# A hybrid attention and MLP block on 8 cores: transposing two spilled operands by crossbar DMA, folding their scales into weights, and loading weights in pieces that wait for TensorE

## The chip, the cores and the metric

One Trainium2 chip, all 8 NeuronCores. Each core takes one batch element's half (every second tile of 128 rows, 2048 query rows), and no core talks to another. The metric is device microseconds of the slowest core; a smaller number is better. Of an execution, the span is the time from the first to the last instruction of the slowest core.

## The reference, cut to what matters

```python
xn = rmsnorm(x, norm_mix_g);  u = xn @ w_in               # 1024 -> 5120
b_g, c_g, v_a, q, k, v, gates = split(u)
y_a = (b_g * conv3(c_g * v_a)) @ w_a_out                   # causal depthwise conv, 512 channels
p = softmax(q k^T / 8 + alibi, causal)                     # 4 heads, two maps of 64 each
o = rmsnorm((p[0] - lam * p[1]) @ v, subln_g) * (1 - lam_init)
y_b = o @ w_b_out
x = x + (sig(gate_a) * y_a + sig(gate_b) * y_b) @ w_o
h = rmsnorm(x, norm_mlp_g) @ w_mlp_in                      # 1024 -> 4096
x = x + square(relu(h)) @ w_mlp_out
return rmsnorm(x, norm_final_g)                            # x is (4, 4096, 1024) float32
```

## The kernel before

Sizes. A core's 4096 rows are eight blocks of 512: blocks 0 to 3 are its own queries, 4 to 7 the other core's rows, needed for k and v. The queries are worked on in four groups g of 512 rows (block g). Weights arrive as float32 and are cast to bf16 by the DMA on POOL's queue (`cload`, `wload`); activations, residual tiles and spills go through SP's queue (`ld` and the stores). Both are in-order queues: an instruction that waits holds what stands behind it.

How the order comes about. Python code records instructions per engine in the order in which it runs; `Sched` adds the waits (last writer, readers) and each engine then executes its list in order. A DMA is an instruction on its issuing engine, with the waits of its source, its destination, and of the DMA 24 places earlier on the same queue.

Stages. First k and v of blocks 4 and 0 and q of block 0 (`until(0)`), which need xT (the transposed x), the weights wk, wv, wq, and the rows' sums of squares (`stats`: ACT squares four x tiles, POOL takes the power). Then the attention loop runs over 160 pairs: group, head, and key tile index j; each pair is 8 q.k matmuls, their exps on ACT and 16 p.v matmuls or fewer. Groups have 16, 32, 48 and 64 pairs. Into this stream `other` puts one chunk of other work per pair from the list W: k, v, q of later blocks, the conv branch, and from the third or fourth pair of group 3 on the gated merge G of groups 0, 1, 2. While attention runs, all of W's chunks share one PSUM bank (`oring` is bank 7); after it there are eight.

The merge of one group i (`G_list`): 32 chunks for 8 output tiles dm (`gate_chunks`: gate 0, branch 0 from y_a, gate 1, branch 1 from the attention output), then the loads for the next group (`g_loads`: xn; `g_loads2`: attention output and y_a), then for each of 4 row tiles two z matmul chunks (`z_chunks`, w_o and the residual). A z of 8 matmuls is followed by L792 on DVE (residual added, x tile loaded by SP), then the copy L795, the square on ACT, and the store of x to xm_sp. After the last pair, what is left of W is worked off alone; at that point the merge of group 1 has its z chunks to do, and groups 2 and 3 all.

Two operands are transposed by TensorE before. The attention output of a head (512 rows x 128) in `epilogue`: step `d3` makes four transposes (L722) of `e_b`, DVE empties them with the scale subln_g folded in (L725), and SP stores the result to on_sp, from where `g_loads2` loads it. The x for the MLP: step `tr` of `z_chunks` makes eight transposes of `g_xb` (L806), DVE empties them with norm_mlp_g folded in (L808), and SP stores them to x2_sp, from where `m_load` loads four pieces.

MLP: 4 blocks, each 32 chunks `m_in` (8 matmuls, W1) and 8 chunks `m_out` (32 matmuls, W2). W1 is loaded into the space of a head's k and v when that head of group 3 is done (two DMAs of 1 MB as written a head, `w1_load`), W2 behind attention and behind the merge in 4 DMAs.

The softmax here doesn't subtract the row's maximum and nothing guards it: scores larger than these inputs give would overflow.

## Time and profile before

| | us |
|---|---|
| median of 3 runs | 1470.52 (1470.09 to 1471.43) |
| profiled execution, device time | 1470.92 |
| its span on the slowest core (core 7) | 1469.4 |
| spans of the 8 cores | 1444.3 to 1469.4 |
| TensorE busy in the span | 1214.9 (83%), 7202 matmuls |
| ACT busy, DVE busy, POOL busy | 546.1, 501.7, 63.2 |
| POOL's DMA queue, SP's DMA queue | 39.91 MB, 76.53 MB as written |

The profile gives for each engine the time it was busy, what it waited for and for how long, and the DMAs with the time from issue to landing. A matmul and its weight load are separate rows (PE and PEld). The granted clock of TensorE is 1.00 at 2.4 GHz and 0.50 at 1.2 GHz; a value between is a mean over a stretch. A wait for several things is put down to the one that came last. The rows that are used are shown further down.

### The profile page before, as it was taken

What the parts mean: (1) busy time and instruction counts of PE and PEld (TensorE: products, weight loads), DVE (VectorE), ACT (ScalarE), POOL (GpSimd) and SP (SyncE); (2) the same over time, 40 slices, a digit from 0 to 9 for tenths busy, and PEclk for the clock granted to TensorE, in tenths of its full rate; (3) what the DMA queues carried; (4) which work ended last, traced back from release to release, by engine and by line L of the source; (5) the groups of instructions that cost most, each with busy time, mean ns of one, the idle gap of its engine ahead of it and who ended that gap; (6) DMA issues with size and microseconds to landing.
All of it is one profiled execution on the core that took longest, in us unless ns stands there. A gap on an engine that the chain in (4) does not pass through costs nothing.

```text
span 1469.4 us, 20538 instructions; the slowest of 8 cores (1444.3 to 1469.4 us)
## 1 busy us (share of the span) xinstructions
PE 1214.9 (83%) x7202; PEld 583.9 (40%) x7202; DVE 501.7 (34%) x1087; ACT 546.1 (37%) x744; POOL 63.2 (4%) x97
## 2 busy tenths in 40 slices
PE   3877687888799872898689629895999999999997
PEld 1333343444444441444344204342444444444443
DVE  2354453553445441324232424543212212212212
ACT  1334264647556561566456102221311311311310
POOL 2001000000000000000000000000000000000000
PEclk8877777999999996999899859998999999999999
DMA  9935113122207107044312561518500200201101
GB/s 172 239 82 103 62 41 97 62 54 65 51 4 148 44 15 147 1 90 124 111 23 68 101 201 32 201 22 208 157 24 35 86 21 38 86 19 40 58 16 56
DMA packets 33124, 117.76 MB, mean 80 GB/s; under 512 B 3680, under 2 KB 8032, under 8 KB 29568
## 3 DMA queue, kind: packets, MB, share of 16 engines
q0 software_dynamic: 7200, 39.91, 16.4%
q1 hardware_dynamic: 25824, 76.53, 15.1%
q8 instruction: 60, 0.98, 0.3%
q14 instruction: 40, 0.33, 0.1%
HBM read 126.98 MB, written 29.36 MB: 106 GB/s over the span
## 4 chain that ended last, share of the span: by engine, by line
PE 68%; DMA 11%; DVE 10%; issue 5%; ACT 4%; POOL 1%; DVEq 0%; SPq 0%; ACTq 0%; POOLq 0%
PE ps_all L396 67%; ACT big L662 3%; DMA x_sp<-big 3%; DMA big<-xs 3%; DMA big<-ya_sp 2%; DMA big<-x_sp 1%; DVE big L769 1%; DVE big L686 1%; DMA on_sp<-big 1%; DMA big<-wk 1%; DVE big L705 1%; PE ps_all L806 1%; DVE big L725 1%; DVE big L714 1%; POOL big L710 0%
## 5 line engine op out<-in xcount | busy, mean ns | idle before, releaser
L396 PE MATMUL ps_all<-big 128*128 128x512 bf16 (+3 forms) x7010 | 1201.0, 338 | 164.6 <-DMA big<-ya_sp 28.9
L396 PEld LDWEIGHTS ps_all<-big 128*128 128x128 bf16 (+1 forms) x7010 | 572.2, 101 | 786.7 <-issue 349.4
L662 ACT ACTIVATE big<-ps_all,big 128x1024 bf16<-128x1024 f32 (+3 forms) x384 | 337.9, 926 | 181.2 <-PE ps_all L396 173.5
L879 ACT ACTIVATE big<-ps_all 128x512 bf16<-128x512 f32 x128 | 76.4, 597 | 141.7 <-PE ps_all L396 141.7
L880 DVE TENSOR_TENSOR big<-big 128x512 bf16<-128x512 bf16 x128 | 54.5, 426 | 159.1 <-ACT big L879 158.8
L758 ACT ACTIVATE big<-ps_all,big 128x512 f32<-128x512 f32 x64 | 44.0, 687 | 151.2 <-PE ps_all L396 151.1
L769 DVE SCALAR_TENSOR_TENSOR big<-big,ps_all 128x512 f32<-128x512 f32 x64 | 44.0, 687 | 156.7 <-PE ps_all L396 156.5
L896 ACT ACTIVATE big<-big 128x1024 bf16<-128x1024 f32 x16 | 16.9, 1057 | 208.2 <-DVE big L891 208.2
L891 DVE SCALAR_TENSOR_TENSOR big<-ps_all,big 128x512 f32<-128x512 f32 x32 | 24.0, 751 | 162.9 <-PE ps_all L396 162.9
L796 ACT ACTIVATE big<-big 128x1024 bf16<-128x1024 f32 x16 | 16.9, 1057 | 128.6 <-DVE big L792 128.6
L806 PE MATMUL ps_all<-big 128*128 128x128 bf16 x128 | 10.9, 235 | 55.0 <-DVE big L795 54.2
L440 ACT ACTIVATE big<-big 128x1024 bf16<-128x1024 f32 x32 | 33.8, 1057 | 52.0 <-DMA big<-xs 51.6
L792 DVE SCALAR_TENSOR_TENSOR big<-ps_all,big 128x512 f32<-128x512 f32 x32 | 22.1, 690 | 80.2 <-DMA big<-xs 47.2
L667 DVE TENSOR_TENSOR big<-big 128x256 bf16<-128x256 bf16 x64 | 18.6, 290 | 71.6 <-ACT big L662 71.2
L710 POOL TENSOR_TENSOR big<-big 128x4 f32<-128x4 f32 x16 | 16.4, 1022 | 512.5 <-DVE big L708 441.3
L548 DVE TENSOR_SCALAR big<-ps_all,big 128x512 bf16<-128x512 f32 x32 | 23.7, 750 | 35.1 <-PE ps_all L396 35.1
L806 PEld LDWEIGHTS ps_all<-big 128*128 128x128 bf16 x128 | 8.4, 105 | 61.4 <-issue 61.4
L598 DVE TENSOR_TENSOR big<-ps_all,big 128x512 f32<-128x512 f32 x16 | 11.1, 691 | 57.0 <-PE ps_all L396 57.0
L722 PE MATMUL ps_all<-big 128*128 128x128 bf16 x64 | 6.5, 228 | 26.5 <-DVE big L714 26.4
L898 POOL TENSOR_TENSOR big<-big 128x1 f32<-128x1 f32 x16 | 8.9, 554 | 435.1 <-DVE big L897 435.1
L669 DVE TENSOR_SCALAR big<-big 128x256 bf16<-128x256 bf16 x64 | 18.2, 285 | 26.0 <-ACT big L662 25.9
L808 DVE TENSOR_TENSOR big<-ps_all,big 128x1024 bf16<-128x1024 bf16 x16 | 19.6, 1225 | 17.8 <-DMA x_sp<-big 10.4
(69 smaller groups left out, 362.8 us busy)
## 6 DMA issues: line engine op xcount, KB each, us to landing
big<-xs SPq DMA_DIRECT2D x48, 512.0 KB, 6.1
big<-w POOLq DMA_DIRECT2D x8, 1024.0 KB, 14.6
xm_sp<-big SPq DMA_DIRECT2D x16, 512.0 KB, 4.5
big<-xm_sp SPq DMA_DIRECT2D x16, 512.0 KB, 5.3
out<-big SPq DMA_DIRECT2D x16, 512.0 KB, 2.7
big<-xT POOLq DMA_DIRECT2D x14, 512.0 KB, 11.0
xn_sp<-big SPq DMA_DIRECT2D x4, 1024.0 KB, 4.9
big<-wg POOLq DMA_DIRECT2D x4, 1024.0 KB, 18.2
```

Source lines behind the costliest of these rows:

```text
L396: S.op("pe", lambda e: e.matmul(out, lhsT, rhs, start=start, stop=stop, skip_group_check=skip), reads, writes)
L440: act(lambda e: e.activation(junk.ap, xt.ap, AF.Square, accum_out=ss1[blk].ap[:, t:t + 1]), [xt], [junk, ss1[blk]])
L548: dve(lambda e: e.tensor_scalar_mul(v_all[:, :, n, 0:128], ps.rearrange("p (h v) -> p h v", h=4), rs1[blk].ap[:, t:t + 1]), [key, rs1[blk] ...
L662: act(lambda e, a=a, b=b, c=c, s=s, PT=PT, scale=scale: e.activation(PT.ap[:, :, a:b], Sb[s][:, :, a:b], AF.Exp, bias=ccol(C_BTAB + c), sc ...
L758: act(lambda e: e.activation(t.ap, ps, AF.Tanh, bias=hbg.ap[:, 8 * w + dm:8 * w + dm + 1], scale=0.5), [key, hbg], [t])
L769: dve(lambda e: e.scalar_tensor_tensor(t.ap, t.ap, 1.0, ps, ALU.add, ALU.mult), [key, t], [t])
L792: dve(lambda e: e.scalar_tensor_tensor(x.ap[:, hs], ps, 0.5, x.ap[:, hs], ALU.mult, ALU.add), [key, x], [x])
L806: S.op("pe", lambda e, c=c: e.transpose(pb[:, c, :], g_xb.ap[:, c * 128:(c + 1) * 128], ident), [g_xb, cbf], [key])
L808: dve(lambda e: e.tensor_tensor(g_x2.ap, pb, ccol(C_GMLP, 8).unsqueeze(2).to_broadcast([128, 8, 128]), ALU.mult), [key, cst], [g_x2])
L879: act(lambda e: e.activation(r.ap, ps, AF.Relu), [key], [r])
L880: dve(lambda e: e.tensor_tensor(h2[fc].ap, r.ap, r.ap, ALU.mult), [r], [h2[fc]])
L891: dve(lambda e: e.scalar_tensor_tensor(x.ap[:, hs], ps, r2q[b].ap[:, t:t + 1], x.ap[:, hs], ALU.mult, ALU.add), [key, x, r2q[b]], [x])
```

## The change

Five things are done, all in one diff.

1. The head's output is no longer transposed in the epilogue: `e_b` (now two buffers) is stored as it is, rows by channels, to on_sp, and `g_loads2` loads it with one transposing DMA on SP (`dma_start_transpose`, 512 x 512 to 128 x 4 x 512). The scale subln_g goes into w_b_out: `fold_sub`, four DVE instructions. `g_on` and `g_ya` have buffers of their own.
2. The MLP's x is no longer transposed in the merge: `g_xb` (two buffers) is stored to xb_sp, and `m_load` is one transposing DMA (512 x 1024 to 128 x 8 x 512). norm_mlp_g goes into W1: 64 DVE instructions, spread over time (`w1_steps`).
3. Weight and xT loads on POOL are cut into halves or quarters, recorded at separate places, and each waits for the matmul that stands last in TensorE's order at that point (`paced`). W2's loads are cut in two-tile pieces, not paced; its first six tiles and `m_load(0)` are recorded in the merge behind attention.
4. The start: the x tiles of blocks 4 and 0 go through POOL's queue in a set order (wk and xT of block 4, x of block 4, wv, xT of 0, wq, x of 0, xT of 5).
5. `g_loads2(0)` is recorded 16 pairs before group 3, in place of at the merge's start; the merge may start at pair 98, before at pair 99. `deferred` steps now also run between the chunks behind attention, and are not flushed at its end.

```diff
@@ Sched
-    def _add(self, eng, fn, reads, writes, is_dma):
-        writers, wars = set(), set()
+    def _add(self, eng, fn, reads, writes, is_dma, extra=(), part=False):
+        writers, wars = set(extra), set()
...
+        self.last[eng] = ev
...
@@ build_program
-    def cload(dst, src, bufs, after=()):
-        S.dma("pool", lambda e: e.dma_start(out=dst, in_=src), reads=after, writes=bufs)
+    def cload(dst, src, bufs, paced=False, part=False):
+
+        S.dma("pool", lambda e: e.dma_start(out=dst, in_=src), writes=bufs, extra=[S.last["pe"]] if paced else (),
+              part=part)
...
         def d2():
-            dve(lambda e: e.tensor_tensor(e_b.ap, o[:, 0, :, 0:128],
+            b = e_b.next()
+            dve(lambda e: e.tensor_tensor(b.ap, o[:, 0, :, 0:128],
                                           est.ap[:, 16:20].unsqueeze(2).to_broadcast([128, 4, 128]), ALU.mult),
-                [o_raw, est], [e_b])
-
-        def d3():
-            ps, key = obank()
...
-                S.op("pe", lambda e, t=t: e.transpose(pb[:, t * 128:(t + 1) * 128], e_b.ap[:, t, :], ident),
-                     [e_b, cbf], [key])
...
+                [o_raw, est], [b])
+            dst = on_sp[g].rearrange("(t p) c -> p t c", p=128)[:, :, h * 128:(h + 1) * 128]
+            S.dma("sp", lambda e: e.dma_start(out=dst, in_=b.ap), [b], ["onsp%d_%d" % (g, h)])
+        deferred.extend([(1, d0), (2, d1), (5, d2)])
...
     def g_loads2(i):
-        ld(span(g_on), on_sp[i], g_on, ["onsp%d_%d" % (i, h) for h in range(4)])
-        ld(span(g_ya), ya_sp[i], g_ya, ["yasp%d_%d" % (i, h) for h in range(4)])
+        ld(g_ya.ap.rearrange("p c t -> p (c t)"), ya_sp[i], [g_ya], ["yasp%d_%d" % (i, h) for h in range(4)])
+        S.dma("sp", lambda e: e.dma_start_transpose(g_on.ap, on_sp[i]),
+              ["onsp%d_%d" % (i, h) for h in range(4)], [g_on])
...
                 if half == 1:
-                    dve(lambda e: e.tensor_copy(g_xb.ap, x.ap), [x], [g_xb])
+                    xb = g_xb.next()
+                    dve(lambda e: e.tensor_copy(xb.ap, x.ap), [x], [xb])
...
+                    S.dma("sp", lambda e: e.dma_start(out=xb_sp[T * 128:(T + 1) * 128, :], in_=xb.ap),
+                          [xb], ["xbsp%d" % T])
...
-        def tr():
...
     def m_load(b):
-        x2 = m_x2[b % 2]
-        for t in range(4):
-            ld(x2.ap[:, t].rearrange("p c t -> p (c t)"), x2_sp[b][t], [x2], ["x2sp%d_%d" % (b, t)])
+        S.dma("sp", lambda e: e.dma_start_transpose(m_x2[b % 2].ap, xb_sp[512 * b:512 * (b + 1), :]),
+              ["xbsp%d" % T for T in range(4 * b, 4 * b + 4)], [m_x2[b % 2]])
...
+    def pieces(bufs, src, c0, width, n=2):
...
+    def xT_steps(blk, s):
+        def first():
+            slot_of[blk] = s
+        steps = [lambda q=q: cload(span(XT[s][2 * q:2 * q + 2]), xT_d[blk][:, 1024 * q:1024 * (q + 1)],
+                                   XT[s][2 * q:2 * q + 2], paced=True) for q in range(4)]
...
-    W += [(0, g_w1)] + [(1, f) for f in conv(3)]
+    W += spread(conv(3), pieces([Wa], wa_d, 0, 4096) + pieces([Wb], wb_d, 0, 4096)
+                + pieces(Wg[0:2], wg_d, 0, 4096) + pieces(Wg[2:4], wg_d, 4096, 4096))
...
-    W += [(1, f) for f in conv(2)] + [(0, g_w2)]
+    W += [(1, f) for f in conv(2)] + [(0, fold_sub)]
     mark("G")
-    W += [(0, lambda: g_loads2(0))]
-    W += G_list(0, 1) + G_list(1, 2) + G_list(2, 3)
+    late = pieces(Wg[4:6], wg_d, 8192, 4096) + pieces(Wg[6:8], wg_d, 12288, 4096) + pieces([Wo], wo_d, 0, 8192, 4)
+    g0 = G_list(0, 1)
+    for k, f in enumerate(late):
+        g0.insert(3 * k, (0, f))
+    W += g0 + G_list(1, 2) + G_list(2, 3)
...
-    def w1_load(h):
+    def w1_steps(h):
+
+        out = []
         for k in (2 * h, 2 * h + 1):
-            cload(W1[k].ap.rearrange("p c n -> p (c n)"), w1_d[:, 4096 * k:4096 * (k + 1)], [W1[k]])
+            out += pieces([W1[k]], w1_d, 4096 * k, 4096)
...
+        due = [(2 + 4 * n, f) for n, f in enumerate(out)]
+        due += [(24 + 2 * n, fold(2 * h + n // 2, n % 2 * 4)) for n in range(4)]
...
+    n_a3 = len(pairs) - 64
     for n, p in enumerate(pairs):
+        if n == n_a3 - 16:
+            g_loads2(0)
...
     oring[0] = Ring(list(range(8)))
+    deferred.extend([(20 + 4 * k, lambda k=k: w2_load(2 * k, 2)) for k in range(3)])
+    deferred.append((36, lambda: m_load(0)))
+    until("G3")
+    until("end")
     run_deferred(True)
-    w2_load(0, 6)
-    m_load(0)
-    until("end")
```

What stands where, at three places. TensorE, from the last attention matmuls (128x129) on. Before, with L722 the attention output's transposes, L806 those of x, and the 512-wide matmuls behind them the merge; it goes on in this way to the MLP's 2048:

```order
L396 MATMUL ps_all<-big 128x129 x8
L396 MATMUL ps_all<-big 128x512 x4
L396 MATMUL ps_all<-big 128x129 x2
L396 MATMUL ps_all<-big 128x512 x8
L396 MATMUL ps_all<-big 128x129 x2
L722 MATMUL ps_all<-big 128x128 x4
L396 MATMUL ps_all<-big 128x512 x28
L806 MATMUL ps_all<-big 128x128 x8
L396 MATMUL ps_all<-big 128x512 x16
```

TensorE at the same place in the changed kernel:

```order
L403 MATMUL ps_all<-big 128x128 x4
L403 MATMUL ps_all<-big 128x129 x8
L403 MATMUL ps_all<-big 128x512 x4
L403 MATMUL ps_all<-big 128x129 x2
L403 MATMUL ps_all<-big 128x512 x8
L403 MATMUL ps_all<-big 128x129 x2
L403 MATMUL ps_all<-big 128x512 x2616
```

The 580 merge matmuls of before (28, 16, 16, 8, 216, 16, 16, 8, 216, 16, 16, 8) with 100 transposes among them have become 568, which stand with the MLP's 2048 in one row without a transpose.

SP at the joint of the merge's groups 2 and 3 (xs: residual tiles; xn_sp, on_sp, ya_sp: the operands of group 3). Before:

```order
L403 DMA big<-xs 128x1024 x2
L403 DMA big<-xn_sp 128x4096
L403 DMA big<-on_sp 128x2048
L403 DMA big<-ya_sp 128x2048
L798 DMA xm_sp<-big 128x1024
L403 DMA big<-xs 128x1024
```

and in the changed kernel, where L843 is the MLP's first x:

```order
L412 DMA big<-xs 128x1024 x2
L843 DMA_TRANSPOSE big<-xb_sp 128x8x512
L412 DMA big<-xn_sp 128x4096
L412 DMA big<-ya_sp 128x2048
L738 DMA_TRANSPOSE big<-on_sp 128x4x512
L793 DMA xb_sp<-big 128x1024
L795 DMA xm_sp<-big 128x1024
L412 DMA big<-xs 128x1024
```

The four loads of the MLP's first x stood at the joint of groups 1 and 2 before; as one transposing load they stand a group later, ahead of the operands of group 3, and the store of x for the MLP stands ahead of that of the residual.

POOL from the conv of group 3 to the merge's first chunks (wa, wb, wg, wo: the merge's weights; L710 and L711 an epilogue's power). Before:

```order
L400 DMA big<-wa 128x4096
L400 DMA big<-wb 128x4096
L400 DMA big<-wg 128x4096 x2
L710 TENSOR_TENSOR big<-big 128x4 x2
L400 DMA big<-wg 128x4096 x2
L400 DMA big<-wo 128x8192
```

and in the changed kernel:

```order
L408 DMA big<-wa 128x2048 x2
L408 DMA big<-wb 128x2048 x2
L711 TENSOR_TENSOR big<-big 128x4
L408 DMA big<-wg 128x2048 x4
L711 TENSOR_TENSOR big<-big 128x4
L408 DMA big<-wg 128x2048 x4
L408 DMA big<-wo 128x2048 x3
```

The same bytes are issued in twice as many DMAs or more, and each of them waits for a matmul.

## Rows read from the trace of the kernel before

**Rows 1.** Stages: length, each engine's busy us (instructions), PEclk, DMA share, GB/s.
```profile
74.00:557.00 483.00, 393.45 (x2818) 201.99 (x2814) 226.74 (x558) 263.41 (x345) 30.96 (x39) 0.87 0.27 64
...
586.00:820.00 234.00, 191.86 (x1488) 98.20 (x1486) 76.99 (x173) 135.20 (x155) 6.39 (x9) 0.94 0.27 66
820.00:1019.00 199.00, 141.75 (x681) 64.53 (x682) 74.55 (x106) 35.79 (x56) 3.71 (x6) 0.85 0.48 132
1019.00:1470.00 451.00, 442.07 (x2049) 200.20 (x2046) 101.63 (x195) 94.48 (x160) 9.39 (x17) 0.99 0.18 56
```

**Rows 2.** Chain that ended last, in order of time: start us, us, what.
```profile
942.66 42.39 PE ps_all L396 x192
...
1019.05 442.04 PE ps_all L396 x2048
```

**Rows 3.** Who waited for whom, whole span: us in total, times, longest us.
```profile
PE ps_all L806 <- DVE big L795: 54.2, 7, 32.4
...
DVE big L792 <- DMA big<-xs: 47.2, 3, 32.4
...
PE ps_all L396 <- DMA big<-ya_sp: 28.9, 1, 28.9
...
PE ps_all L722 <- DVE big L714: 26.4, 12, 7.9
...
PE ps_all L396 <- ACT big L662: 15.3, 26, 1.7
...
PE ps_all L396 <- DVE big L808: 10.5, 3, 8.0
PE ps_all L396 <- DVE big L725: 9.5, 14, 0.7
```

**Rows 4.** Timeline around 557 us: start, us, engine, instruction [idle before, releaser].
```profile
552.16 1.27 POOL L400 DMA_DIRECT2D big<-wg  x2 [20.06 <-PE ps_all L396]
...
553.42 0.54 POOL L400 DMA_DIRECT2D big<-wo  x1
...
557.48 0.32 SPq L403 DMA_DIRECT2D big<-ya_sp  x1
```

**Rows 5.** DMA issues from 545 to 590 us: KB each, us to landing.
```profile
big<-wo POOLq DMA_DIRECT2D x1, 2048.0 KB, 30.9
...
big<-ya_sp SPq DMA_DIRECT2D x1, 512.0 KB, 27.8
```

**Rows 6.** Timeline from 800 to 880 us, TensorE and SP.
```profile
822.72 0.59 PE L722 MATMUL ps_all<-big 128*128 128x128 bf16 x4 [7.86 <-DVE big L714]
...
837.39 18.28 SPq L403 DMA_DIRECT2D big<-x_sp  x4
...
872.46 1.01 PE L806 MATMUL ps_all<-big 128*128 128x128 bf16 x8 [32.39 <-DVE big L795]
```

**Rows 7.** Timeline of ACT from 0 to 100 us.
```profile
60.13 1.06 ACT L440 ACTIVATE big<-big 128x1024 bf16<-128x1024 f32 x1 [3.53 <-DMA big<-xs]
...
74.14 5.84 ACT L662 ACTIVATE big<-ps_all,big 128x512 bf16<-128x512 f32 x8 [1.99 <-PE ps_all L396]
```

**Rows 8.** The stretch behind the hole at 557 us, columns as in Rows 1.
```profile
580.00:600.00 20.00, 13.31 (x96) 6.86 (x96) 2.29 (x4) 8.55 (x13) 0.00 (x0) 0.76 0.20 54
```

**Rows 9.** Groups by line: busy us, mean ns of one, idle before and releaser.
```profile
L806 PE MATMUL ps_all<-big 128*128 128x128 bf16 x128 | 10.9, 235 | 55.0 <-DVE big L795 54.2 <-DVE big L725 0.7
...
L523 DVE TENSOR_SCALAR big<-big 128x512 bf16<-128x512 bf16 x24 | 7.4, 347 | 18.6 <-DMA big<-xs 11.2 <-DMA big<-wk 7.5
L722 PE MATMUL ps_all<-big 128*128 128x128 bf16 x64 | 6.5, 228 | 26.5 <-DVE big L714 26.4
```

**Rows 10.** DMA issues of the whole span: KB each, median us to landing.
```profile
big<-w POOLq DMA_DIRECT2D x8, 1024.0 KB, 14.6
...
big<-xn_sp SPq DMA_DIRECT2D x4, 1024.0 KB, 6.3
...
big<-x_sp SPq DMA_DIRECT2D x16, 256.0 KB, 2.6
```

More of the change, by code:

```diff
@@ L451, in build_program @@
     slot_of = {}
-    def xT_load(blk, s, pieces=2):
-        slot_of[blk] = s
-        n = 8 // pieces
-        for q in range(pieces):
-            wload(XT[s], xT_d[blk], q * n, n, 512)
     def stats(blk, nxt):
@@ L929, in build_program @@
         k_evac(4, h, *ps4[h])
+    for f in stats(4, None):
+        f()
+    for t in range(4):
+        tok_pool(0, t)
+    for q in range(2):
+        wload(XT[2], xT_d[5], 4 * q, 4, 512)
     for c in range(8):
```

167 lines of the change are left out of this document (79 added, 88 removed).

## The prediction, made before the changed kernel ran

> **What bounds the kernel now.** I read the stages first. [rows 1] cuts the span of the slowest core at the joints of the program: the attention passes (74 to about 815 us), a tail in which only the gated merge is left (815 to 1019), and the MLP (from 1019). The MLP is 2048 matmuls in 442.04 us [rows 2], 216 ns each at a granted clock of 0.99: nothing waits there and nothing of it can be won without removing matmuls. Before it TensorE is also the longest chain, but with holes. So I read next what TensorE waits for [rows 3]. The large entries are few: 54.2 us in front of the transposes of x (L806), 28.9 us for one load of ya_sp, 26.4 us in front of the transposes of the attention output (L722), 10.5 us behind L808, which empties the transposed x, and 9.5 us behind L725, which empties the transposed attention output. Then I looked at why these come late. At 552 us POOL issues two wg loads and wo, 4 MB as written and 8 MB as read, in one go; the two loads that the first branch needs stand behind them and ya_sp lands 27.8 us after its issue [rows 4, 5]. At 837 us SP's sequencer stands for 18.28 us on four x_sp loads, each behind a store, with the merge's own loads queued after them; the residual x comes 32 us late (DVE's longest wait for xs in [rows 3]), and because the transposes stand in TensorE's own order between the z matmuls, TensorE stops too, 32.39 us [rows 6]. So the losses are transfers that collide, and TensorE being chained to what the vector engine does with them.
>
> **Startup.** The first exp comes at 74.14 us, 14 us after the last tile of block 0's rows arrives for its square at 60.13 [rows 7]. By then six loads of 2.1 MB (three weights, three xT) and eight x tiles (4.2 MB) stand in front: 16.8 MB. In the new order xT of block 5 stands after block 0's tiles, so 14.7 MB stand in front: 2.1/16.8 of 58 us is 7 us. Bounds: 0, because block 5's squares on ACT still stand ahead of the first exp and their tiles now share the queue with two xT loads; 14, if all that wait went. I take 7.
>
> **Attention, 74 to 815 us.** (a) The 28.9 us for ya_sp go: the loads of group 0 are now issued 18 pairs before their use, and a pair takes about 4.2 us (56 pairs in the 234 us of [rows 1]), so 75 us cover even a 28 us load. (b) After that hole the clock is at 0.76 over 20 us [rows 8]: 48% of the stretch at the lower level, so of 13.3 us of matmuls 6.4 ran at half speed; 3 us come back. (c) Fifteen of the sixteen output transposes lie here: waits 26.4 less 7.9 for the last [rows 3, 6] = 18.5, the evictions 9.5, the matmuls 15/16 of 6.5 [rows 9] = 6.1. (d) x's transposes of one group: 10.5 behind L808 and a quarter of 10.9. Together (c) and (d) are 47.3 us. Not all returns: TensorE's next instruction often waits for an exp (L662, 26 waits, 15.3 us), and while TensorE stood at a transpose ACT got ahead. The bounds are 0 and 47; I take 80%, 38, since most of these holes are longer than the 0.6 us that a wait for L662 is on average. (e) What is new: at the joint of two groups SP carries, in order, xn (1 MB, 6.3 us), ya (512 KB), the transposing load of the attention output (512 KB, time X), then the next x tile (512 KB). A plain 512 KB load is 3.8 us on the line between 2.6 and 6.3 [rows 10], so the tile is there after 13.9 + X. With one PSUM bank for this work, cover is four pairs, 16.8 us: a stall of X - 2.9. Sum: 28.9 + 3 + 38 - 2.1 = 68 gained.
>
> **X**, the crossbar load, is the unknown: no row of before has one. From below it is a plain load, 3.8 us; from above the slowest load of this size that the trace has, 27.8 us behind 4 MB of others [rows 5]. I take 5, near the plain row, because the bytes and the engines are the same and the 27.8 were spent in a queue that the change empties.
>
> The Trainium skill weighs in on both sides here. Its page "DMA: Bandwidth & Descriptors", section "Latency and other measured facts", gives 261 GB/s for a transposing DMA with a non-contiguous middle dimension, by which X would be an estimated 2 us plus a start and the sum would come out as I have it. Its page "VectorE: DVE Perf Modes", section "The three transpose paths", gives 1309 ns for one 128x128 tile by the crossbar; by that, sixteen tiles one after another make an estimated X of 21 us and the sum about 1414. No row of before tells which holds.
>
> **The tail.** From the last attention matmul (822.72 - 7.86 = 814.9 us, [rows 6]) to the MLP at 1019.05 are 204.2 us. There are 580 merge matmuls and 100 transposes in it now; in the new order it is 568 matmuls in one unbroken row. At the undisturbed rate, 192 in 42.39 us [rows 2], 568 take 125.4 us. On top: at the joint of groups 1 and 2 SP's loads need 13.9 + X = 18.9 us, and TensorE, with eight banks, can run 64 z matmuls and 24 more before it must have a bank back, 88 x 0.221 = 19.4 us: no stall, were it not for the last head's MLP weights in the same stretch, of which two halves are in flight (a whole one lands in 14.6 us, [rows 10]); 0 to 15, I take 4. At the joint of groups 2 and 3 the MLP's x (1 MB, 2X) goes ahead of all this: 13.9 + 3X - 19.4 = 9.5. At the MLP's start, W2 comes in as before and x tiles wait; DVE's waits for xs beside the longest are 47.2 - 32.4 = 14.8 us [rows 3], TensorE can now run some 56 matmuls past them (12.4): 2.5 remain. 2 us for a colder clock. 125.4 + 18 = 143.4: 61 gained.
>
> **At no cost.** W1's scales are folded by 64 vector instructions of 347 ns (the kind of L523, [rows 9]) = 22 us, in place of L725 and L808; DVE is busy 77 of 234 us there [rows 1]. If a W1 half came late, DVE would stand and with it the evictions; the fold stands five pairs, 21 us, after the last half's issue. The paced loads make POOL wait for a TensorE instruction; behind that stand the next loads and the small pow of an epilogue, whose reader comes three half pairs (6 us) later. One xT piece stands directly ahead of its reader, block 7's k: 0 to 4 us, once; taken as nothing, since a pair of 4.2 us lies between. The output's store now has 256-byte runs, off any path: its reader comes a group later. The MLP itself stays at 450 us.
>
> **Sum.** 7 + 68 + 61 = 136. Against the profiled execution, 1470.9 (the median is 1470.5): 1335 us.
>
> **Rivals.** First, the waits move instead of vanishing: in attention ACT's exps (135 of 234 us busy) or the single bank take the place of the transposes, and of (c) and (d) nothing returns: 1335 + 38 = 1373. For it: L662 already stands behind 26 waits. Against: TensorE is at 82% and the exps at 58% [rows 1]. 15%. Second, the pieces don't do what they say: a paced load still collides with the merge's loads, and a hole like that at 557 stays somewhere, 1335 + 29 + 3 = 1367. For it: the bytes are the same. Against: POOL now can't run ahead of TensorE. 9%. Third, the crossbar load is several times a plain one. The three joints cost (X - 2.9) + (X - 5.5 + 4) + (3X - 5.5) and 15.6 of it is in my sum, so it adds 5X - 25.5; at X = 16, the middle of the two bounds, 1335 + 55 = 1390. 17%. Fourth, on the other side, the same mechanism further out: the addition reaches 136 at X = 32 us, a little above the slowest plain load; at X = 40 it is 174 and the kernel takes 1509. 6%; it decides from X = 32 on.
>
> **How the numbers follow.** The forecast has 53%. Its own range takes the bounds: startup 0 to 14, attention from 30 less to 9 more, tail 18 more to 11 less, that is 1305 to 1380. The whole range must reach the first and second rivals and most of the third, up to about X = 20: 1303 to 1410. A measurement of this kernel tells about 0.2% (3 us) from no change. Faster: all but the fourth and a little of the third beyond 1467, 93%; same 1%; slower 6%.
>
> **What will show it.** Right: no wait of TensorE over 5 us between 75 and 800 us; first exp near 67; the transposing loads landing in 4 to 7 us (512 KB) and 8 to 12 (1 MB); the last attention matmul near 740; then 568 matmuls in 130 to 145 us and the MLP's 442 unchanged. Wrong: a crossbar load over 10 us, SP standing at it, and z evictions waiting for xs at the joints; or TensorE's waits for L662 grown from 15 to over 40 us; or a hole at the first branch again.

## The result, and the profile after

The changed kernel takes 1339.56 us (median; 1337.55 to 1342.04) beside 1470.97 us for the kernel before on the same chip: a ratio of 0.9107, 95% interval 0.909 to 0.9124. The forecast was 1335 us, range 1303 to 1410. Its total was 4.6 us off; two of its three terms were off by more, in opposite directions. Every ratio below is to the kernel before in the same set of runs and leaves disturbed executions out.

Line numbers shift with the change: L403 is the matmul (L396 before), L663 the exp (L662), L786 the addition of the residual x to z (L792), L763 the branch, L738 the transposing load of the attention output, L843 that of the MLP's x, L447 a square of the startup, L524 a fold of a norm scale into a weight.

The stages of the slowest core (busy us and instruction counts of each engine, the granted TensorE clock, the share of the DMA engines), from the first exp to about the last attention matmul and from there to the end. First the kernel before:

```profile
74.00:815.00 741.00, 585.79 (x4306) 300.43 (x4302) 299.89 (x718) 399.83 (x501) 37.35 (x48) 0.88 0.30 69
815.00:1470.00 655.00, 583.82 (x2728) 264.73 (x2728) 180.01 (x315) 130.96 (x217) 13.11 (x23) 0.95 0.27 79
```

Then the kernel after:

```profile
70.00:731.00 661.00, 554.57 (x4220) 287.50 (x4220) 305.64 (x750) 400.19 (x502) 51.50 (x75) 0.94 0.38 82
731.00:1338.00 607.00, 574.40 (x2624) 257.93 (x2622) 169.36 (x319) 129.41 (x216) 20.51 (x37) 0.97 0.32 83
```

By these cuts attention is 80 us shorter, the rest 48, the startup 4. (The last attention matmul of the kernel after ends 2.7 us behind the cut at 731; to it the attention stage is 78 us shorter.) The stage is not only less idle (155 us of TensorE's time before, 106 after): TensorE's busy time fell too, by 31 us for 86 fewer instructions, at a granted clock of 0.94 where it was 0.88. Core 7 of the kernel before is one of two cores at 0.88; over the cores whose matmuls are all on record, six in each kernel, the busy time fell by some 21 us, and part of that is the transposes that are gone.

What TensorE waits for in the kernel after (us in total, times, longest us), the answer to [rows 3]:

```profile
PE ps_all L403 <- DVE big L786: 23.8, 5, 9.2
PE ps_all L403 <- DMA big<-xT: 20.0, 5, 11.0
PE ps_all L403 <- DVE big L763: 17.4, 20, 2.6
PE ps_all L403 <- ACT big L663: 15.5, 31, 1.7
```

The waits in front of the transposes and for ya_sp are gone. The wait for exps is 15.5 us, where [rows 3] has 15.3; that for xT lies in the startup but for 2.3 us. The largest entry is now the z addition, L786, and 18.9 of its 23.8 us stand in the tail. TensorE's timeline of the tail (start us, us, then in brackets the idle time before the row and what ended it):

```profile
730.40 23.54 PE L403 MATMUL ps_all<-big 128*128 128x512 bf16 x102 [2.58 <-DVE big L763]
760.16 37.77 PE L403 MATMUL ps_all<-big 128*128 128x512 bf16 x163 [6.21 <-DVE big L786]
798.15 55.41 PE L403 MATMUL ps_all<-big 128*128 128x512 bf16 x256 [0.23 <-DVE big L766]
853.79 19.37 PE L403 MATMUL ps_all<-big 128*128 128x512 bf16 x89 [0.23 <-DVE big L766]
876.68 5.30 PE L403 MATMUL ps_all<-big 128*128 128x512 bf16 x16 [3.52 <-DVE big L786]
891.16 69.07 PE L403 MATMUL ps_all<-big 128*128 128x512 bf16 x311 [9.18 <-DVE big L786]
```

The last two stops stand behind the MLP's first matmul, which starts at 866.1 us (counted back from the last of its 2048). From the last attention matmul to that place it was 204.0 us before and is 132.4 now. The MLP's matmuls, from the first to the last, take 458.7 us where they took 442.2.

Behind L786 stands DVE's own wait, for x tiles, in total about as long as the 47.2 us in 3 waits of [rows 3]:

```profile
DVE big L786 <- DMA big<-xs: 46.7, 4, 14.9
```

But the places differ. Before, 32.4 us stood in the middle of the tail and 14.4 at the MLP's start; after, 7.5 stand in attention, 12.2 in the middle of the tail, and 14.9 and 12.1 at the MLP's start. There W2 arrives. In the kernel before, a load of 12 of its tiles was issued at 984.72 us, and one of the last two x tiles came late; in the kernel after, two bursts of four pieces, 16 tiles in all, meet both of them. The x tiles' size and their time to landing in this place, before and after, and POOL's two bursts:

```profile
big<-xs SPq DMA_DIRECT2D x1, 512.0 KB, 18.5
big<-xs SPq DMA_DIRECT2D x2, 512.0 KB, 17.7
851.73 2.11 POOL L408 DMA_DIRECT2D big<-w  x4 [20.19 <-PE ps_all L403]
866.80 2.12 POOL L408 DMA_DIRECT2D big<-w  x4 [12.95 <-PE ps_all L403]
```

The end of the program grew too: from the last matmul to the end of the span it is 12.4 us, and was 8.3. POOL's last instruction is a DRAIN, and the program ends 0.2 us after it (the line; its ns as min, median and max; its start), before and after:

```profile
L156 POOLq DRAIN  x1: 4144/4144/4144, 1465.0 to 1465.0; - x1
L165 POOLq DRAIN  x1: 8304/8304/8304, 1328.7 to 1328.7; - x1
```

Before, it is over within 0.2 us of SP's own DRAIN, which follows SP's wait for the last store; after, it ends 4.5 us behind that. It takes 4.14 us where POOL has issued 50 DMAs, 8.30 in the changed kernel with 101, and 6.59 with 80, in the run below that has most weights in whole loads. So some 4 us is the price of more DMAs on POOL; 8 of the 51 more are the startup's x tiles, the others are pieces.

The DMA issues that answer to [rows 10] (KB each where known, median us from issue to landing). The first row is the kernel before's, of the plain load of the attention output that the crossbar load replaces; the others are the kernel after's:

```profile
big<-on_sp SPq DMA_DIRECT2D x4, 512.0 KB, 7.9
big<-xn_sp SPq DMA_DIRECT2D x4, 1024.0 KB, 6.7
big<-ya_sp SPq DMA_DIRECT2D x4, 512.0 KB, 7.3
big<-on_sp SPq DMA_TRANSPOSE x4, 8.7
big<-xb_sp SPq DMA_TRANSPOSE x4, 11.0
```

So X, the unknown of the prediction, is 8.7 us for 512 KB, not 5, and 11.0 for 1 MB (over the eight cores the medians are 7.1 to 8.9 and 9.9 to 11.9; the plain load of before has 5.9 to 8.2). A transposing load also holds SP's sequencer, as its timeline shows (start us, us that the issue took); a plain load there takes 0.33 us:

```profile
727.79 4.68 SPq L738 DMA_TRANSPOSE big<-on_sp  x1
764.27 23.58 SPq L843 DMA_TRANSPOSE big<-xb_sp  x1
795.64 0.33 SPq L412 DMA_DIRECT2D big<-xn_sp  x1
796.69 6.38 SPq L738 DMA_TRANSPOSE big<-on_sp  x1
858.67 0.56 SPq L412 DMA_DIRECT2D big<-xs  x1
871.78 0.33 SPq L412 DMA_DIRECT2D big<-xs  x1
```

### The profile page after: what moved, and what is told of

Same layout as the page of the kernel before. It is cut to its first block, busy times and chain, and to the rows that moved or that the text cites. A ratio compares the mean times of both kernels' runs of the same rounds, so it can differ in the third digit from the quotient of the medians.

```text
span 1337.2 us, 20332 instructions; the slowest of 8 cores (1316.2 to 1337.2 us)
## 1 busy us (share of the span) xinstructions
PE 1171.1 (88%) x7010; PEld 562.7 (42%) x7010; DVE 497.2 (37%) x1123; ACT 544.9 (41%) x744; POOL 90.2 (7%) x148
## 2 busy tenths in 40 slices
DMA packets 67411, 117.74 MB, mean 88 GB/s; under 512 B 37072, under 2 KB 39376, under 8 KB 66288
## 3 DMA queue, kind: packets, MB, share of 16 engines
q0 software_dynamic: 14544, 44.11, 20.6%
## 4 chain that ended last, share of the span: by engine, by line
PE 72%; DVE 8%; DMA 8%; ACT 5%; issue 5%; POOL 1%; DVEq 0%; SPq 0%; ACTq 0%; POOLq 0%
PE ps_all L403 72%; ACT big L663 4%; DMA big<-xs 3%; DMA big<-wv 2%; DVE big L763 1%; DMA xm_sp<-big 1%; DVE big L687 1%; DMA big<-xhT 1%; POOL big L408 1%; DVE big L700 1%; DVE big L549 0%; DVE big L786 0%; DVE big L689 0%; DVE big L599 0%; DVE big L608 0%
## 5 line engine op out<-in xcount | busy, mean ns | idle before, releaser
L403 PE MATMUL ps_all<-big 128*128 128x512 bf16 (+3 forms) x7010 | 1171.1, 333 | 153.7 <-DVE big L786 23.8
L403 PEld LDWEIGHTS ps_all<-big 128*128 128x128 bf16 (+1 forms) x7010 | 562.7, 100 | 761.6 <-issue 292.4
L663 ACT ACTIVATE big<-ps_all,big 128x1024 bf16<-128x1024 f32 (+3 forms) x384 | 338.8, 929 | 149.5 <-PE ps_all L403 138.2
L763 DVE SCALAR_TENSOR_TENSOR big<-big,ps_all 128x512 f32<-128x512 f32 x64 | 43.7, 686 | 109.7 <-PE ps_all L403 109.0
L447 ACT ACTIVATE big<-big 128x1024 bf16<-128x1024 f32 x32 | 33.9, 1058 | 48.6 <-DMA big<-xs 47.9
L786 DVE SCALAR_TENSOR_TENSOR big<-ps_all,big 128x512 f32<-128x512 f32 x32 | 22.1, 691 | 74.2 <-DMA big<-xs 46.7
L711 POOL TENSOR_TENSOR big<-big 128x4 f32<-128x4 f32 x16 | 16.7, 1043 | 322.1 <-DVE big L709 322.1
L408 POOL DMA_DIRECT2D big<-w x32 | 17.5, 555 | 200.3 <-PE ps_all L403 173.5
L670 DVE TENSOR_SCALAR big<-big 128x256 bf16<-128x256 bf16 x64 | 18.2, 285 | 25.5 <-ACT big L663 25.5
L700 DVE SCALAR_TENSOR_TENSOR big<-big 128x128 f32<-128x128 f32 x64 | 22.5, 352 | 7.2 <-DVE big L700 0.5
L1020 DVE TENSOR_SCALAR big<-big 128x512 bf16<-128x512 bf16 x64 | 22.5, 352 | 5.3 <-DVE big L670 0.2
L766 DVE TENSOR_TENSOR big<-big 128x512 bf16<-128x512 f32 x32 | 22.2, 692 | 3.3
```

What stands on the lines that cost most here:

```text
L403: S.op("pe", lambda e: e.matmul(out, lhsT, rhs, start=start, stop=stop, skip_group_check=skip), reads, writes)
L408: S.dma("pool", lambda e: e.dma_start(out=dst, in_=src), writes=bufs, extra=[S.last["pe"]] if paced else (), part=part)
L447: act(lambda e: e.activation(junk.ap, xt.ap, AF.Square, accum_out=ss1[blk].ap[:, t:t + 1]), [xt], [junk, ss1[blk]])
L663: act(lambda e, a=a, b=b, c=c, s=s, PT=PT, scale=scale: e.activation(PT.ap[:, :, a:b], Sb[s][:, :, a:b], AF.Exp, bias=ccol(C_BTAB + c), sc ...
L700: dve(lambda e, t=t: e.scalar_tensor_tensor(o[:, 0, t, 0:128], o[:, 0, t, 0:128], rl[:, 0, t:t + 1], o[:, 1, t, 0:128], ALU.mult, ALU.add) ...
L763: dve(lambda e: e.scalar_tensor_tensor(t.ap, t.ap, 1.0, ps, ALU.add, ALU.mult), [key, t], [t])
```

## The experiments

Two questions were open. Which part carries the attention stage's gain, and does the crossbar, now slower than I took it, cause what is left in the tail? The first set undoes one part at a time; the second separates pacing from the order of two loads; the third takes an improvement apart and tests the startup. The table has, from each profiled execution, the time of the first exp, the time from there to the end of the last exp, and from there to the end of the core's span, each a mean over the eight cores, so that it isn't one core's luck.

| kernel | profiled us | ratio to before (95%) | first exp | exps | rest |
|---|---|---|---|---|---|
| before | 1470.9 | 1 | 74.2 | 729.8 | 652.9 |
| after | 1338.9 | 0.9107 (0.909 to 0.9124) | 68.2 | 652.8 | 606.0 |
| after, again in the second set | 1334.4 | 0.9112 (0.9069 to 0.9155) | 67.7 | 651.4 | 603.1 |
| plain loads for the crossbar's | 1342.1 | 0.9149 (0.9081 to 0.9216) | 68.4 | 655.9 | 607.1 |
| attention output on TensorE | 1380.0 | 0.9381 (0.9302 to 0.946) | 68.1 | 692.9 | 601.5 |
| x on TensorE | 1367.0 | 0.927 (0.9227 to 0.9313) | 67.8 | 658.1 | 629.7 |
| no pacing | 1348.7 | 0.9197 (0.9124 to 0.927) | 71.3 | 657.1 | 606.8 |
| late ya, paced | 1347.2 | 0.9173 (0.9127 to 0.9219) | 67.3 | 660.4 | 605.8 |
| late ya, whole, unpaced | 1379.4 | 0.9383 (0.9339 to 0.9427) | 71.3 | 684.3 | 609.8 |
| x first and late W2 | 1308.6 | 0.8908 (0.8873 to 0.8944) | 68.0 | 649.4 | 584.5 |
| x first | 1318.2 | 0.8951 (0.8891 to 0.9011) | 67.8 | 651.1 | 591.2 |
| late W2 | 1322.2 | 0.9024 (0.8967 to 0.9081) | 68.2 | 651.7 | 592.9 |
| x first, late W2, folds first | 1310.2 | 0.8891 (0.8815 to 0.8967) | 67.8 | 650.8 | 584.4 |
| xT of block 5 ahead of the tiles | 1348.1 | 0.9153 (0.9075 to 0.9232) | 73.3 | 655.0 | 606.1 |

### What does the crossbar itself cost?

```
-        S.dma("sp", lambda e: e.dma_start_transpose(g_on.ap, on_sp[i]),
+        S.dma("sp", lambda e: e.dma_start(out=g_on.ap.rearrange("p c t -> p (c t)"),
+                                          in_=on_sp[i].rearrange("(p a) d -> p (a d)", a=4)),
...
-        S.dma("sp", lambda e: e.dma_start_transpose(m_x2[b % 2].ap, xb_sp[512 * b:512 * (b + 1), :]),
+        S.dma("sp", lambda e: e.dma_start(out=m_x2[b % 2].ap.rearrange("p c t -> p (c t)"),
+                        in_=xb_sp[512 * b:512 * (b + 1), :].rearrange("(p a) d -> p (a d)", a=4)),
```

> Both kinds of transposing loads become plain loads of the same bytes into the same buffers, so the attention output and the MLP's x arrive untransposed and the output is another one; everything else as in the changed kernel. Theory (the prediction's sum, in which each joint pays for the crossbar load in SP's queue): the transposing loads land in 8.7 us (512 KB) and 11 to 27 us (1 MB) where plain ones take 4 to 7, so by the formula 5 X the time falls by some 20 to 25 us, to about 1317. Rival (the crossbar loads lie beside other work and TensorE's stalls in the tail come from x tiles that share the DMA engines with the W2 pieces): less than 8 us, 1332 to 1340, and the z evictions wait for xs as long as before.

The ratio is 0.9149 (0.9081 to 0.9216) where the changed kernel has 0.9107: nothing gained, against the 20 to 25 us that I expected by my formula, and 1342.6 us is just past the rival's 1340. The rows say why. The plain loads' landing times, in the same places:

```profile
big<-xb_sp SPq DMA_DIRECT2D x4, 1024.0 KB, 7.6
big<-on_sp SPq DMA_DIRECT2D x4, 512.0 KB, 9.0
```

A plain 512 KB load takes 9.0 us there, as long as the transposing one (8.7); over the cores the medians are 6.3 to 9.0, against 7.1 to 8.9. Both stand behind 1.5 MB issued just ahead of them, which I take for the reason; no run had the load in an empty queue. The 1 MB load is 3.4 us faster and is issued early enough to hide either. SP no longer stands, and TensorE still stops in the same place, for longer:

```profile
767.88 0.33 SPq L843 DMA_DIRECT2D big<-xb_sp  x1
763.77 37.38 PE L403 MATMUL ps_all<-big 128*128 128x512 bf16 x160 [10.56 <-DVE big L786]
PE ps_all L403 <- DVE big L786: 28.4, 5, 10.6
```

So the crossbar doesn't set the time of this kernel, and the tail's remaining stops aren't its doing. As the plain load came no sooner, the run does not test what the formula says of a faster one.

### The attention output back on TensorE

```
-        deferred.extend([(1, d0), (2, d1), (5, d2)])
+        def d3():
+            ps, key = obank()
+            pb = ps.bitcast(BF16)[:, 0:512]
+            for t in range(4):
+                S.op("pe", lambda e, t=t: e.transpose(pb[:, t * 128:(t + 1) * 128], e_b.ap[:, t, :], ident),
+                     [e_b, cbf], [key])
+            dve(lambda e: e.tensor_copy(e_o.ap, pb), [key], [e_o])
+            S.dma("sp", lambda e: e.dma_start(out=on_sp[g][:, h * 512:(h + 1) * 512], in_=e_o.ap), ...
+        deferred.extend([(1, d0), (2, d1), (4, d2), (5, d3)])
```

> The attention output is transposed by TensorE again (four transposes, an eviction by VectorE and a store of 1 KB runs per head), its load is a plain one; the rest as in the changed kernel. Theory: of the 34.1 us of waits and busy time that the prediction counted for these transposes within attention some 80% return, 27 us, and the last head's 8 us in the tail, less some 4 us that the plain load saves at the joints: about 1365 to 1372. Rival (the waits move to the exps, so the crossbar buys nothing here): 1335 to 1345, with TensorE's waits for the exps at 15 us in both.

The exps take 692.9 us instead of 652.8: 40 us, more than the theory's 27, and the profiled 1380.0 lies above the 1365 to 1372 expected. The waits that came back, and the stage of its slowest core (the columns are those of the stage rows above):

```profile
PE ps_all L724 <- DVE big L716: 19.1, 9, 3.7
PE ps_all L404 <- DVE big L726: 9.3, 15, 0.7
70.00:775.00 705.00, 579.42 (x4272) 297.33 (x4272) 310.51 (x763) 399.80 (x502) 51.74 (x75) 0.91 0.34 76
```

Against the changed kernel's 661 us there are 44 us more on this core. Idle time is 705 - 579.4 = 125.6 against 661 - 554.6 = 106.4, so 19 us of the 28.4 us of waits really lengthen the stage, as some of it was time in which TensorE would have waited for an exp (L664 fell to 12.7 us). The transposes' own busy time in the stage is 6.8. The other 18 us are the other matmuls running slower: the granted clock is 0.91 over the stage instead of 0.94. This core has the lowest clock of the eight. Over the six cores of each run whose matmuls are all on record the 40 us are 22 of idle time, 7 of transposes and 12 of slower matmuls, at 0.93 instead of 0.95. So many short stops, one or two at every head, cost through slower matmuls about half of what they cost through the waiting, and on the slowest core nearly as much.

### The MLP's x back on TensorE

```
+        def tr():
+            ps, key = obank()
+            pb = ps.bitcast(BF16).rearrange("p (c t) -> p c t", c=8)
+            for c in range(8):
+                S.op("pe", lambda e, c=c: e.transpose(pb[:, c, :], g_xb.ap[:, c * 128:(c + 1) * 128], ident), ...
+            dve(lambda e: e.tensor_copy(g_x2.ap, pb), [key], [g_x2])
...
+            out.append((1, zs[t][1]))
+            if t >= 1:
+                out.append((0.3, zs[t - 1][3]))
+            out.append((1, zs[t][2]))
```

> The MLP's x is transposed by TensorE again, one tile behind its z matmuls, and loaded by four plain loads; the rest as in the changed kernel, the norm scale folded into W1 included. Theory: TensorE is again chained to the z evictions, so the 13.2 us of (d) return in attention and most of the 54.2 us in the tail where the x tiles come late, in all 30 to 50 us: 1370 to 1390. Rival (the late x tiles of before came from whole-size loads that collided, and pacing has removed these): only the transposes' own busy time, 128 of 0.085 us = 11 us, and their evictions' waits of some 10 us: 1350 to 1362.

The ratio is 0.927 against 0.9107: 0.0163 of 1471 us is 24 us, and the profiled execution is 28 us longer, 5 of them in the exps and 24 in the rest by the table. That is just short of the theory's 30 to 50 and just past the rival's 1362. TensorE's waits in the tail of this kernel:

```profile
PE ps_all L801 <- DVE big L790: 29.5, 7, 8.7
```

It waits 29.5 us in front of the transposes, where [rows 3] had 54.2 over the kernel. So the other parts of the change had already taken about half of that wait, and the crossbar takes what was left.

### Pacing, size and order of the loads

```
-        S.dma("pool", ..., extra=[S.last["pe"]] if paced else (),
+        S.dma("pool", ..., extra=(),
```

> Weight pieces keep their size and their place in the order but POOL no longer waits for TensorE before it issues them. Theory (pacing removes the hole at the first branch): pieces are issued as soon as their buffer is free, the loads of the joint meet them again, and a hole of 10 to 29 us comes back between 500 and 800 us: 1350 to 1370. Rival (the earlier issue of ya and of the attention output for group 0 is what removed the hole, and pacing only spreads what would have landed in time anyway): 1335 to 1345 with no wait over 5 us.

Without pacing alone, POOL issues each head's W1 pieces in one go, and the profiled execution takes 1348.7 us:

```profile
613.41 2.20 POOL L408 DMA_DIRECT2D big<-w  x4
686.89 2.20 POOL L408 DMA_DIRECT2D big<-w  x4
```

No wait for ya_sp came back, so the hole that the theory named is not there, though the time is nearer to its 1350 to 1370 than to the rival's 1335 to 1345. The interval of the ratio, 0.9124 to 0.927, doesn't tell this from no change or from 20 us. By the table 3 of the 10 us of the profiled execution are in the startup and 4 in the exps. The next two put the loads of ya and of the attention output for group 0 back to the head of its merge, once paced and once with whole loads and no pacing, beside the changed kernel on the same chip.

```
-        if n == n_a3 - 16:
-            g_loads2(0)
...
     mark("G")
+    W += [(0, lambda: g_loads2(0))]
```

> The changed kernel itself, as the measure beside which the other three of this set stand on the same chip. Expected: 1335 to 1345.

> The loads of ya and of the attention output for group 0 are issued directly at the head of group 0's merge again, as before the change, not 18 pairs earlier; weight pieces stay small and paced. Theory (the hole of 28.9 us came from the 4 MB that were issued in one go ahead of them, and pacing alone takes most of it): ya lands within 8 us and the attention output in 8 more, a gate covers some 6 us: a stall of 5 to 10 us at the first branch, 1345 to 1350. Rival (the early issue is what took the hole away): a hole of 20 us or more stays, 1360 to 1370.

```
     def pieces(bufs, src, c0, width, n=2):
+        n = 1
...
-        S.dma("pool", ..., extra=[S.last["pe"]] if paced else (),
+        S.dma("pool", ..., extra=(),
```

> As the run with the late ya loads, but each weight goes in one whole load and POOL does not wait for TensorE. Theory (pieces and pacing carry the gain): the hole at the first branch is back at about its old 29 us, so some 20 us above the paced one: 1360 to 1375. Rival (the order of the loads matters, not their size or pacing): within 4 us of the paced run.

TensorE's wait for ya_sp, first of the paced one, then of the one with whole loads and no pacing:

```profile
PE ps_all L403 <- DMA big<-ya_sp: 6.0, 1, 6.0
```

```profile
PE ps_all L403 <- DMA big<-ya_sp: 28.6, 1, 28.6
```

The second is the hole of the kernel before to within a third of a us (28.9 in [rows 3]). The exps take 684.3 - 651.4 = 33 us longer, that is the hole and little else: TensorE's busy time there, over the cores with a full record, is 552.2 us against 551.5, though the granted clock, a mean over the stretch with the hole in it, is 0.925 against 0.947. With pacing 6.0 us of the hole stay, and 9 us in the exps. The two kernels lie 32 us apart, more than the theory's 20, and the second, at 1378 us, is above its 1360 to 1375. Of the 43 us that the mean of the cores has between it and the changed kernel some 4 are in the startup and 7 behind the exps. So the early issue (with small pieces, unpaced) removes this hole, and paced pieces without the early issue remove four fifths of it; the changed kernel has both, which is why the run without pacing alone shows so little. Whole loads with the early issue were not tried, nor small pieces without pacing at the late issue, so the size of the pieces and the pacing are not told apart.

### x tiles first, W2 late

If the z addition waits for x tiles that share the DMA engines with weights and with the next group's 2 MB, these are to be moved, not the transposes.

```
-        out += gates[:24] + [(0, zs[0][0]), (0, zs[1][0])] + gates[24:]
+        out += gates[:24] + [(0, zs[t][0]) for t in range(3)] + gates[24:]
...
-            if t + 2 < 4:
-                out.append((0, zs[t + 2][0]))
+            if t == 0:
+                out.append((0, zs[3][0]))
...
-            cload(span(W2[f:f + 2]), w2_d[:, 1024 * f:1024 * (f + 2)], W2[f:f + 2])
+            cload(span(W2[f:f + 2]), w2_d[:, 1024 * f:1024 * (f + 2)], W2[f:f + 2], paced=f0 >= 6)
```

> Two stalls that stay in the changed kernel are attacked: each group's third x tile is loaded ahead of the next group's 2 MB instead of behind them, and the last 20 W2 tiles wait for the last z matmul. Theory (TensorE's 23.8 us behind the z eviction come from x tiles that share the DMA engines with weights and with the next group's loads): the stall in the middle of the tail (6 to 10 us) and those at the MLP's start (3.5 and 9.2 us) go for the most part: 15 us less than the changed kernel on the same chip, about 1325. Rival (the tiles are late because their buffer comes free late, a store of 512 KB after the tile before): less than 4 us.

1308.74 us (median; 1306.44 to 1310.27) beside 1338.62 for the changed kernel on the same chip: 30 us less, twice the 15 expected, and no kernel of this study is clearly faster. The edit holds back 26 W2 tiles, all behind the first six, not 20. The tail of its slowest core is one row of matmuls without a stop for L786:

```profile
725.27 58.72 PE L403 MATMUL ps_all<-big 128*128 128x512 bf16 x265 [2.58 <-DVE big L763]
784.22 55.41 PE L403 MATMUL ps_all<-big 128*128 128x512 bf16 x256 [0.23 <-DVE big L766]
839.86 120.38 PE L403 MATMUL ps_all<-big 128*128 128x512 bf16 x557 [0.23 <-DVE big L766]
727.00:1307.00 580.00, 566.89 (x2621) 256.39 (x2619) 169.49 (x318) 129.92 (x216) 20.45 (x37) 0.99 0.33 85
```

Of the 27 us between this stage row and that of the changed kernel (607), 7.5 are busy time again, at a clock of 0.99 instead of 0.97. The mean core gains less, 20 us in all: in the changed kernel the last stop, 8 to 10 us that end at 888 to 891, stands on four of the eight cores, and they are its four slowest (1334 to 1337 us, the others 1316 to 1325). That the transposing load holds SP matters still less here than before; this row of the same kernel stood for 46.71 us, while the W2 tiles landed, and TensorE, in an unbroken row until at least 960 us, didn't wait for it:

```profile
857.73 46.71 SPq L843 DMA_TRANSPOSE big<-xb_sp  x1
```

Then each half alone (of the edit above, the first two hunks, and the third).

> Half of the run with x tiles first and late W2: only the third x tile of each group is loaded ahead of the next group's loads. Both halves together took 30 us off the changed kernel, twice what TensorE's waits for the z evictions had suggested on its slowest core. Theory: each half takes its own stall, this one those at the joints in attention and in the middle of the tail (some 5 and 6 us, and the colder clock behind them): 10 to 15 us, 1325 to 1330. Rival: nearly all comes from the W2 loads: within 4 us of the changed kernel, 1335 to 1340.

> The other half: only the last 20 W2 tiles wait for the last z matmul. Theory: the stalls of 3.5 and 9.2 us at the MLP's start go, with the colder clock behind them: 13 to 18 us, 1322 to 1327. Rival: the x tiles there wait for the store that frees their buffer, so the stalls stay: 1335 to 1340.

TensorE's timeline of the one with x tiles first, and then two rows of the one with W2 late:

```profile
726.84 58.72 PE L403 MATMUL ps_all<-big 128*128 128x512 bf16 x265 [2.58 <-DVE big L763]
869.98 90.32 PE L403 MATMUL ps_all<-big 128*128 128x512 bf16 x408 [5.73 <-DVE big L786]
```

```profile
760.49 37.24 PE L403 MATMUL ps_all<-big 128*128 128x512 bf16 x163 [7.18 <-DVE big L786]
853.60 106.57 PE L403 MATMUL ps_all<-big 128*128 128x512 bf16 x493 [0.23 <-DVE big L766]
```

Each half takes its own stop: the early tile that at about 754, the late W2 those at 873 to 891. The early tile also shortens the latter, as group 3's tiles are then ahead of W2; so it is worth more than I had expected (1318.2 where 1325 to 1330 was expected), and late W2 alone somewhat less (a median of 1328.3, expected 1322 to 1327). In the table's last column the halves give 12 and 10 us off 603.1, both together 19.

### The startup

```
-    W += spread(ks(0) + vs(0), [lambda c=c: fold_gain(Wq, c) for c in range(8)])
-    W[-12:-12] = [(0, f) for f in stats(0, 5)]
+    W += spread(ks(0), [lambda c=c: fold_gain(Wq, c) for c in range(8)])
+    W += [(0, f) for f in stats(0, 5)]
+    W += [(1, f) for f in vs(0)]
```

> The run with x tiles first and late W2, and in the startup the folds of Wq stand ahead of VectorE's wait for block 0's sums of squares instead of behind it. Theory (the startup gained less than the 7 us predicted because VectorE stands from about 50 to 57 us and the folds and k evictions queue behind that): the first exp comes about 6 us earlier, at 64 to 65 us instead of 70.6: 1300 to 1304. Rival (the end of the startup is set by the arrival of Wq and of block 0's xT): no change, 1306 to 1311.

The theory fell: the first exp comes at 67.8 us (mean), as before this edit (68.0), and the ratios agree. ACT's timeline of its slowest core shows what took the folds' place (idle time before a row in brackets):

```profile
63.16 1.06 ACT L447 ACTIVATE big<-big 128x1024 bf16<-128x1024 f32 x1 [2.09 <-DMA big<-xs]
68.70 1.06 ACT L447 ACTIVATE big<-big 128x1024 bf16<-128x1024 f32 x1 [3.09 <-DMA big<-xs]
69.76 5.82 ACT L663 ACTIVATE big<-ps_all,big 128x512 bf16<-128x512 f32 x8
```

The exp no longer waits for TensorE; it starts the moment ACT has squared a tile of block 5, which stands ahead of it and came late. Two limits lie close together here: in the changed kernel's slowest core ACT was done with these squares at 68.96 us, 1.6 us ahead of its first exp.

```
+    for q in range(2):
+        wload(XT[2], xT_d[5], 4 * q, 4, 512)
     for f in stats(4, None):
         f()
     for t in range(4):
         tok_pool(0, t)
-    for q in range(2):
-        wload(XT[2], xT_d[5], 4 * q, 4, 512)
```

> The changed kernel with one part of its startup put back: xT of block 5 (2 MB as read) is issued ahead of block 0's x tiles. Theory (the term of 7 us in the prediction: 2.1 of 16.8 MB no longer stand ahead of the tiles): block 0's last square, and with it the first exp, comes 7 us later, 1343 to 1347. Rival (the loads share the engines all the same, or other waits cover it): less than 3 us.

The first exp comes at 73.3 us, 5.1 later than in the changed kernel, and the profiled execution takes 1348.1. The ratio's interval, 0.9075 to 0.9232, is too wide to show this in the total, but all eight cores have their first exp between 72.7 and 73.9, where the changed kernel has them between 66.5 and 70.6. Block 0's last square starts at 60.5 us before, 53.7 in the changed kernel and 58.8 here (means of the cores), and the first exp follows it by 14.5 us on every core of the latter two. So one order of two loads carries most of the startup's gain. Pacing has a part as well: without it the first exp comes at 71.3 us, directly behind ACT's last square of block 5, which then starts at 70.3 instead of 65.6.

## Why the prediction was right, and where it wasn't

**Startup, 7 predicted.** 6.0 us in the mean of the cores (74.2 to 68.2), 3.5 between the two slowest cores (74.14 in [rows 7], 70.58 after). The mechanism is shown by the run with block 5's xT ahead, and its size by block 0's last square, which comes 6.8 us earlier. That ACT's squares would keep the rest was the reason for the lower bound, and the runs with the folds first and without pacing show ACT there.

**Attention, 68 predicted.** 77 us in the mean of the exps (729.8 to 652.8), 78 on the slowest cores. By terms: (a) and (b), the hole at the first branch and its clock, were 31.9; putting the hole back costs 33, under 1 of it in slower matmuls where (b) had 3. That step is right in the main. (c) and (d) were 80% of 47.3 us, 38; the two transposes put back cost 40 and 5 us in the exps, 45 together. The discount itself holds: of the 28.4 us of waits for the attention output's transposes 19 on the slowest core, 22 in the mean, lengthen the stage. The step that failed is that I counted the clock only for the one long hole of [rows 8]. The short stops lower it over the whole stage, and that is worth another 12 us in the mean, 18 on the slowest core. (e), the joint of groups 0 and 1, was 2.1; TensorE stops there for 4.7 us on the slowest core and under 3 on the others, and moving an x tile ahead there is worth under 2 in the exps.

**X, 5 us predicted.** 8.7 us measured, 11.0 for 1 MB, above what I took and far from the upper bound. By the prediction's own formula, 5 X - 25.5, this would have added 18 us. At two of the three joints the formula is not far off: X - 2.9 and X - 1.5 are 5.8 and 7.2, and the stops are 4.7 and 6.21. At the third, 3 X - 5.5 = 20.6, there is none: the MLP's x was issued at 764.27 us, 31 us ahead of that joint's loads, and had landed 27.2 us later, before they went out. And nothing is to be had by a plain load: in the same place it takes 9.0. The failed step is that I priced the load by rows from other places ([rows 10], 2.6 to 6.3 us), with less ahead of them in the queue. The same listing of the kernel before had the plain load of the attention output itself, 7.9 us, and I passed it over. The Trainium skill's page "DMA: Bandwidth & Descriptors", section "Latency and other measured facts", gives a rate from which an estimate of some 2 us plus a start follows, and "VectorE: DVE Perf Modes", section "The three transpose paths", a time for one tile, from which 21 us follow as an estimate for tiles one after another. Neither is what a load takes here; that sixteen tiles land in 8.7 us, queue included, speaks against the second as a price for a load of many tiles.

**Tail and MLP, 61 predicted.** 47 us in the mean (652.9 to 606.0), 51 on the slowest cores from the last attention matmul on. The merge came out better than forecast: 132.4 us from the last attention matmul to the MLP's first, where I had 143.4. TensorE does run in one row past the transposes, as said, and the joint of groups 2 and 3, for which I had 9.5 us, costs nothing; the joint of groups 1 and 2 has 6.21 where I had 4. What failed is the MLP's start and "The MLP itself stays at 450 us". For the start I had 2.5 us: 14.8 of DVE's waits, less a cover of 12.4. The cover was about right, 27.0 us of waits less 3.52 + 9.18 of stops being 14.3. The waits were not: I took them over from before, but two x tiles are late there now and not one, since the W2 pieces come in beside both. With a colder clock behind the stops the MLP's matmuls take 16.5 us more than before. The run with late W2 has no stop there. The run with x first and late W2 shows that some 20 us of the rest hung on these two orders. Another 4 us is POOL's DRAIN at the end, which no term had.

**At no cost.** The folds of W1, the paced waits and the store in 256-byte runs cost nothing to be seen: in none of these profiles does TensorE wait longer than 1.4 us at a time for a fold of W1. That the pieces cost nothing is wrong by the DRAIN's 4 us.

**The rivals.** Waits that move to the exps: no, 15.5 us for 15.3. Pieces that don't do what they say: no hole at the first branch, and a whole one when they are undone together with the order. A crossbar of several times a plain load: its time is nearly double what I took, but no more than a plain load's in its place. The slower side had the same mechanism and fell with it. That the total of 136 us came out so closely (1470.9 to 1338.9 is 132) is luck in part: 9 to 10 us too little in attention and 10 to 14 too much in the tail cancel.

## What to carry to other kernels

Price a transfer by a row from the place in the program where it will stand, not by the fastest row of its size: the row of the very load that is replaced was nearest to the truth here, and plain and transposing loads took about the same. Count short stops that recur twice, once as waiting and once as slower matmuls around them; the busy column of two stage rows, with equal instruction counts, shows the second. The mean granted clock alone does not, as it also falls with idle time: one hole of 28.6 us lowered it from 0.947 to 0.925 and the matmuls took the same time. And when a wait is gone, look at what it waited for: the x tiles were late as ever in total, only in another place, and loading them ahead of what nobody needed yet gave another 30 us.

## What the runs showed of the hardware

- A transposing DMA holds the sequencer that issues it: 3.8 to 10.3 us over the cores of the changed kernel, where a plain load takes 0.33, and 20 to 24 us for its first 1 MB load, issued together with four weight pieces; 46.71 us while W2 was landing in the kernel with x first and late W2. A plain load can stand too: 17.82 us for three x tiles in that kernel, 751 us into its span.
- It moves its data in small packets: 37072 packets under 512 bytes in the changed kernel, 12368 with plain loads. The difference of 24704 for 6 MB is about 255 bytes each. The total number of bytes, 117.74 MB, is the same.
- Matmuls run slower where TensorE stops often. With a stop or two at each head's end the attention stage ran at a mean granted clock of 0.93 of 2.4 GHz, without them at 0.95, and its other matmuls took 12 us longer; the tail without its three stops ran at 0.99 instead of 0.97.
- POOL's DRAIN at the program's end grows with the number of DMAs that POOL has issued: 4.14 us for 50, 6.59 for 80, 8.30 for 101, some 0.08 us each.
